# Six native fp32 gate panels in a hybrid mixer block, instead of three native and three split

## The reference, cut to what matters

```python
h = rms_norm(x, g_mix)
proj = h @ w_in                                   # 1024 x 5060
u_ssm, q, k, v, qi, ki, wi, qm, gates = jnp.split(proj, offs, axis=-1)
...
y_ssm = s5_branch(...); y_dsa = dsa_branch(...); y_mem = memory_branch(...)
g_s, g_d, g_m = jnp.split(jax.nn.sigmoid(gates), 3, axis=-1)
merged = g_s * (y_ssm @ w_up_ssm) + g_d * (y_dsa @ w_up_dsa) + g_m * (y_mem @ w_up_mem)
x = x + merged @ w_out
x = x + hier_moe(rms_norm(x, g_ffn), ...)         # 32 experts, top 2
```

## Time and profile before

| | |
|---|---|
| median of 3 runs | 2053.33 us (2052.51 to 2055.39) |
| the profiled execution, its time | 2054.06 us |
| its span, first to last instruction | 2052.2 us |
| TensorE busy | 1892.3 us |
| VectorE busy | 1189.7 us |
| ScalarE busy | 820.0 us |
| mean granted clock of TensorE | 0.967 |

### The profile page before, as it was taken

The page is one execution under the profiler, slowest core; times in us unless marked ns, Lnnn a source line. Parts: engine busy times, 40 slices in busy tenths (PEclk is TensorE's granted clock), DMA queues, the critical chain, the costliest instruction groups (busy, mean ns, idle before and its releaser), DMA issues.

```text
span 2052.2 us, 29797 instructions
## 1 busy us (share of the span) xinstructions
PE 1892.3 (92%) x12272; PEld 1419.6 (69%) x12272; DVE 1189.7 (58%) x1495; ACT 820.0 (40%) x1016; POOL 90.0 (4%) x79
## 2 busy tenths in 40 slices
PE   7988998877787787799999999999999999999998
PEld 5335666544444444588898778888888898788887
DVE  6998745533333343654578566555655688385554
ACT  4215442222222121543357475333533368465332
POOL 2670000000000000000000000000000000000000
PEclk9999999899999889899999999999999999999999
DMA  7223337799999999555454444554564544455643
GB/s 251 90 82 123 124 105 303 300 420 420 420 420 420 421 419 416 188 185 194 150 178 168 163 144 160 190 205 144 205 205 167 182 166 148 140 168 175 211 164 103
DMA packets 160440, 453.40 MB, mean 221 GB/s; under 512 B 9600, under 2 KB 21120, under 8 KB 135728
## 3 DMA queue, kind: packets, MB, share of 16 engines
q1 hardware_dynamic: 158480, 447.65, 59.2%
q10 hardware_dynamic: 1616, 3.24, 0.5%
q0 software_dynamic: 208, 0.59, 0.1%
HBM read 544.78 MB, written 1.05 MB: 266 GB/s over the span
## 4 chain that ended last, share of the span: by engine, by line
PE 72%; DMA 17%; DVE 7%; ACT 2%; issue 1%; POOL 1%; SPq 0%; ACTq 0%; DVEq 0%; POOLq 0%
PE ps L992 23%; PE ps L1002 17%; PE ps L1001 17%; DMA ring<-in_w_down 12%; DMA ring<-in_w_up 4%; PE ps L1160 3%; PE ps L1465 2%; PE ps L1483 2%; PE ps L1444 1%; DVE xn L2454 1%; PE ps L1128 1%; PE ps L1129 1%; DVE W L2459 1%; DVE W L2461 1%; DVE xn L2448 1%
## 5 line engine op out<-in xcount | busy, mean ns | idle before, releaser
L2270 DVE TENSOR_TENSOR w_lo<-raw,w_hi 128x2048 fp32r<-128x2048 f32 (+2 forms) x153 | 336.1, 2208 | 135.4 <-ACT w_hi L1757 128.3
L1757 ACT ACTIVATE w_hi<-raw 128x2048 fp32r<-128x2048 f32 (+2 forms) x153 | 281.6, 1849 | 226.8 <-PE ps L992 189.9
L1002 PE MATMUL ps<-w_hi,a_lo 128*128 128x512 f32 (+1 forms) x984 | 371.5, 378 | 0.0
L992 PE MATMUL ps<-w_hi,a_hi 128*128 128x512 f32 (+1 forms) x936 | 356.8, 381 | 0.2 <-DVEq L2310 0.2
L1001 PE MATMUL ps<-w_lo,a_hi 128*128 128x512 f32 (+1 forms) x928 | 349.5, 377 | 0.0
L1465 PE MATMUL ps<-ring,W 128*32 128x256 f32 x3008 | 191.0, 402 | 60.2 <-DMA ring<-in_w_up 60.2
L1002 PEld LDWEIGHTS ps<-w_hi,a_lo 128*128 128x128 f32 x984 | 185.1, 188 | 34.5
L992 PEld LDWEIGHTS ps<-w_hi,a_hi 128*128 128x128 f32 x936 | 176.2, 188 | 33.2 <-issue 2.1
L1001 PEld LDWEIGHTS ps<-w_lo,a_hi 128*128 128x128 f32 x928 | 174.8, 188 | 30.8
L1465 PEld LDWEIGHTS ps<-ring,W 128*32 128x32 f32 x3008 | 95.8, 114 | 142.0 <-DMA ring<-in_w_up 68.8
L2270 DVE TENSOR_TENSOR y_lo<-raw,y_hi 128x2048 fp32r<-128x2048 f32 x51 | 116.9, 2291 | 51.9 <-ACT y_hi L1757 49.1
(11 more groups left out here) (436 smaller groups left out, 2857.3 us busy)
## 6 DMA issues: line engine op xcount, KB each, us to landing
ring<-in_w_gate SPq DMA_DIRECT2D x94, 1024.0 KB
ring<-in_w_up SPq DMA_DIRECT2D x94, 1024.0 KB
ring<-in_w_down SPq DMA_DIRECT2D x94, 1024.0 KB
raw<-in_w_in SPq DMA_DIRECT2D x56, 1024.0 KB, 5.1
raw<-in_ffn_w_gate SPq DMA_DIRECT2D x44, 1024.0 KB, 5.1
raw<-in_ffn_w_up SPq DMA_DIRECT2D x44, 1024.0 KB, 5.1
raw<-in_ffn_w_down SPq DMA_DIRECT2D x40, 1024.0 KB, 5.9
raw<-in_w_out SPq DMA_DIRECT2D x9, 1024.0 KB, 5.1
```

What stands on the lines that cost most here:

```text
L992: return released(pe.matmul(dst, a, b, skip_group_check=True, **kw))
L1002: return pe.matmul(dst, a_l, b_h, start=False, stop=final, skip_group_check=True)
L1757: act.activation(E.hi_view(name, ahead), E.raw_view(name, ahead), ACT.Copy).then_inc(hi_split, 1)
L2270: tt(E.lo_view(name, ahead), E.raw_view(name, ahead), E.hi_view(name, ahead).bitcast(F32), ALU.subtract)\
```

## The change

gate(1), gate(4) and gate(5) are computed natively, from raw weights and `a_full`. Their six units are neither rounded nor subtracted, and `g_hi`, `g_lo` and the signal `gate_rows` are gone. The panels of `w_out` stay split.

```diff
-PRE_SPLIT = [(n, kh) for n in [("gate", c) for c in (1, 4, 5)] + [("wo", c) for c in range(2)] for kh in range(2)]
+PRE_SPLIT = [(n, kh) for n in [("wo", c) for c in range(2)] for kh in range(2)]
...
-    mark("gate_rows", "hi", "lo")
...
-        g_hi, g_lo = y_lo[:, 0:2].rearrange("p a k s -> p (a k) s"), a_lo
...
             def gate(c):
                 fills = [("gate", c, t) for t in range(2)]
-                if (("gate", c), 0) in PRE_SPLIT:
-                    pe.wait_ge(done["gate_rows"], nth("gate_rows", "lo"))
-                    rows_panel(halves(("gate", c)), fills, (g_hi, g_lo))
-                else:
-                    raw_rows(halves(("gate", c)), fills)
+                raw_rows(halves(("gate", c)), fills)
...
-            act.wait_ge(unit_used, E.unit_value(("vm", 1)) + 1)
-            act.wait_ge(done["turned"], nth("turned", ("x", 1, 1)))
-            act.activation(g_hi, a_full[:, :, :], ACT.Copy).then_inc(done["gate_rows"], 1)
-            act.wait_ge(done["gate_rows"], nth("gate_rows", "hi"))
-            hi1((("gate", 1), 0))
-            hi1((("gate", 1), 1))
             for h in range(2):
                 act.wait_ge(done["gelu_in"], nth("gelu_in", h))
...
-            hi1((("gate", 4), 0))
-            hi1((("gate", 4), 1))
             gate(2)
...
-            hi1((("gate", 5), 0))
             exponentials("dsa", 1, probs, 0, 8)
-            hi1((("gate", 5), 1))
             gate(4)
...
-            dve.wait_ge(done["gate_rows"], nth("gate_rows", "hi"))
-            tt(g_lo[:, :, :], a_full[:, :, :], g_hi.bitcast(F32), ALU.subtract).then_inc(done["gate_rows"], 1)
-            dve.wait_ge(done["gate_rows"], nth("gate_rows", "lo"))
-            lo1((("gate", 1), 0))
-            lo1((("gate", 1), 1))
             dve.wait_ge(done["rstd"], nth("rstd", "heads1"))
...
-            lo1((("gate", 4), 0))
-            lo1((("gate", 4), 1))
             normalised("dsa", 0, 4, probs, 0)
             selected(1)
             row_maxima("dsa", 1, 4, 0.125, key_bias, probs, 0)
-            lo1((("gate", 5), 0))
             normalised("dsa", 1, 4, probs, 0)
             attended("dsa", 0, 1)
-            lo1((("gate", 5), 1))
```

More of the change, by code:

```diff
@@ L65 @@
 SIGNALS = ("meansq rstd rows gained turned_hi turned ssm_act ssm_vec ssm_params ssm_weights trig angle rope_angle "
-           "rope_trig u_rows scanned rotated mixed gate_rows gelu_in gelu evacuated heads heads_turned values "
+           "rope_trig u_rows scanned rotated mixed gelu_in gelu evacuated heads heads_turned values "
            "relued maxed exped probs probs_turned branch gates residual route_in route silu hidden "
```

## The result

The changed kernel takes 2063.52 us, median of 5 runs (2062.87 to 2064.75), the kernel before 2053.75 us, median of 5: a ratio of 1.0048, 95% interval 1.0033 to 1.0062. It is slower by 9.8 us, 6.8 to 12.7 by the interval; 8.2 us were forecast, and the range of 2058.0 to 2065.5 us holds the median.

The account below looks back on a forecast made before the run. TensorE was taken to bound the kernel from 159 to 322 us; three native panels add 2.67 + 2.77 + 2.79 = 8.2 us, removed work nothing, giving 2061.5 us for the median, range 2058.0 to 2065.5.

Parts of the forecast that it names:

- TensorE sets the stage, and the delay goes to the end: From 159 to 322 us a TensorE microsecond more is one later; the expert stage can't absorb the 8.2 us.
- The case in which the delay is swallowed: Rival: the expert stage, bound by transfers from 373 us, takes the delay in; 2053.3 us, chance 0.06.
- The price of a panel: gate(1), gate(4), gate(5) native at 13.79 us each against 11.12, 11.02, 11.00 split: 8.2 us more.
- The estimate from the Trainium skill: Panels priced from the pages: native 13.8 us, split 10.4 us, so 3.5 us a panel and 10.4 in all.
- The removed work is worth nothing: 13.2 us less on ScalarE and 15.9 us less on VectorE bring no gain, as neither is awaited there.
- The clock: Rival on slips at TensorE's gaps: one vanishing gives 2060 us, two added 2065; two or more added, chance 0.06.
- The other side (faster): Rival: VectorE sets the pace at 192.60 and 230.95 us, up to 11.3 us back; 2050.2 us, chance 0.02.
- gate(0)'s row of 15.62 us: Upper bound for a native panel: gate(0) at a granted clock of 0.55 at first, costing 1.8 us more.
- gate(4) follows dense work: Reason for 13.79 us, the full-clock row: gate(1), gate(4) and gate(5) all follow dense TensorE work.
- the first scores' slip: Slow clock at 196 to 200 us, 16 matmuls in 3.53 us against 2.00; its vanishing would return 1.5 us.
- its four gaps: TensorE waits of 1.9, 1.5, 2.0 and 0.5 us, each ended by a ScalarE copy, expected to stay.
- the least that can be told from none: For the whole kernel: a change under 0.2% (4.1 us) can't be told from none.

Follow-up runs that it names:

- filled pair: Kernel before and changed kernel, both with extra unread TensorE products at the same six gaps: split 2047.59 us, native 2057.03 us (11 runs each).
- experiment 2: Kernel before with gate(1), gate(4), gate(5) native but all split work kept and waited for: 2063.05 us, ratio 1.0048.
- experiment 3: Kernel before, gate(4) and gate(5) using gate(1)'s rounded units, their own four neither rounded nor subtracted, still three products: 2053.97 us, ratio 0.9998.
- experiment 5: The changed kernel run again beside more runs of the kernel before: 2063.11 us (5 runs) beside 2053.39 (21 runs), ratio 1.0051.
- plain pair: The kernel before and the changed kernel, both without extra products in TensorE's gaps: 2053.75 and 2063.52 us, ratio 1.0048.
- experiment 8: Kernel before with four more units split (second and third branch's projections up): 2050.98 us, ratio 0.9984; with gaps filled too, 2045.81 us, ratio 0.9965.
- experiment 4: Changed kernel with seven extra TensorE products in some gaps (turned heads, dsa_scores(0), routing's ranks): 2063.46 us, ratio 1.0045.
- experiment 1: Kernel before with gate(4) alone native, its two units neither rounded nor subtracted: 2056.60 us (11 runs) beside 2053.98, ratio 1.0016.
- experiment 7: Kernel before and changed kernel, each with extra TensorE products at the same six gaps: split 2047.59 us, ratio 0.9979; native 2057.03 us, ratio 1.0017.

## Why the prediction was right, point by point

- **TensorE sets the stage, and the delay goes to the end: right.** TensorE is 9.7 us late at gate(5)'s end, and so is the first expert load; the token rows are 10.9 us late, the products behind the experts 10.9, the end 10.8. The case in which the delay is swallowed is out.
- **The price of a panel: right to 0.1 us, the sum short by a quarter of a microsecond.** 13.74, 13.84 and 13.74 us against 13.79 forecast. What the sum left out is the hand-over: gate(1) and gate(5) start 0.2 and 0.1 us later after the start of the group ahead of them when they are native (6.90 for 6.72 us, 1.75 for 1.66); gate(4) does not. From the start of glu to gate(1)'s end it is 17.84 and 20.64 us, from the turned memory heads to gate(5)'s end 12.66 and 15.49, and gate(4) 11.02 and 13.84: 2.80 + 2.83 + 2.82 = 8.45 us (glu and heads start at 174.76 and 251.35 before, at 175.04 and 258.19 after). The filled pair shows 8.4. The estimate from the Trainium skill ("FP8 and Floating Point Precision", TensorE Precision Notes, and "TensorE: Matmul & The Clock Gate", Back-to-back issue gap), 10.4 us, was too high: it counts a split product at 215.8 ns where gate(4)'s 48 take 11.02 us, 230 ns each. That section of the Trainium skill gives this figure for the gap of a single matmul, and about 131 ns for a sustained stream of weight loads and matmuls of 512 columns; no run here shows 131 ns.
- **The removed work is worth nothing: right,** by the list of waits and by experiments 2 and 3. The slack grew as forecast: the turned q heads are ready at 182.9 us and asked for at 195.68, 12.8 us instead of 9.3; the first half's probabilities at 231.2 and 234.99, 3.8 instead of 3.4.
- **The clock: the term that was mis-sized.** The forecast let the slips stand as they were, with one either way. In the profiled pair the changed kernel lost 0.3 us more in gate(0), 0.9 in the scores and 1.2 in the routing, 2.4 us beside the panels' 8.45; that makes the 10.8. With the gaps filled, the stretch from gate(0) to w_out shows the panels' price alone. So the excess in this stretch is the clock's. Set against its length at the full clock, 161.73 us split and 170.13 native, each plain profile has a loss of its own:

  | profile | gate(0) to the last turned part | over the full clock |
  |---|---|---|
  | before, split | 164.31 | 2.6 |
  | experiment 3, split | 164.77 | 3.0 |
  | experiment 2, native | 172.10 | 2.0 |
  | changed, native | 173.95 | 3.8 |
  | experiment 5, native | 174.10 | 4.0 |

  The two executions of the changed kernel in this table are the slowest and all but the slowest of their five runs, and that of experiment 2 is the fastest of its five, so the table shows what can happen and not an average. By the means the plain pair is 10.2 us apart, with a standard error of about 0.4 us (estimated from the scatter of the runs), which is more than the panels' 8.45; the filled pair is 8.5 apart. So the changed kernel does lose more to the clock, by some 2 us, in the stretch and in the routing together, and the forecast had no term for it beyond one slip either way. Why it does stays open. The native form alone doesn't bring it: the smallest loss is that of a native execution, and in experiment 8 a split one, whose TensorE does up to gate(4) what the kernel before does, had all three groups of scores slow.
- **The other side (faster): out.** Experiment 3 took 9.1 us from VectorE and 7.6 from ScalarE, and no gain shows (at most 2.3 us by its interval).
- **Smaller slips of the prediction.** It sets gate(0)'s row of 15.62 us, with its drain, against 13.79 from start to start; from start to start gate(0) took 15.46, so the low clock cost 1.7 us there and not 1.8. It says that gate(4) follows dense work; gate(4) follows 16 small matmuls of 2.00 us behind a gap of 1.97, and in experiment 4 the low clock reached into it (14.26 us). It prices the first scores' slip at 1.5 us; experiment 1 without it was 0.9 us shorter there, because the next gap grew from 1.49 to 2.08 us. One of its four gaps is ended by the relu (L1913), not by a copy. And it takes 4.1 us as the least that can be told from none, where experiment 8 told 2.4 us with 11 runs beside 21.

## What to carry to other kernels

Three rounded products (fp32r) cost TensorE 0.69 us for a 128x128 by 128x512 block and a native fp32 product 0.86 us: leaving the split out frees the other engines and charges TensorE a quarter more, so where TensorE sets the pace it can pay only if a rounding or remainder is what TensorE waits for. Ask at each handover who arrives last; here VectorE was 3.4 and 9.3 us early, and splitting four more units gained 2.4 us. When a forecast rests on rows of one execution, look for stretches of theirs at the lower clock, and give each one a price both ways, with what the next gap gives back. To compare two forms, take a stretch that ran at the full clock in both.

## What the runs showed of the hardware that was not expected

- The granted clock fell under or just ahead of small matmuls behind TensorE gaps of 1.5 to 2.0 us in some executions and not in others: 16 score matmuls took 2.00 us or up to 3.79 us. Where a gap was filled with products that nobody reads, the score matmuls behind it took 2.00 us in all five profiles with extra products; in experiment 4 the clock fell at the next open gap.
- Filling can backfire: products put in after the clock has fallen run at the slow rate (eight instructions of 512 columns in 4.82 us for 3.70, and in the routing in 5.26) and may end after the wait that they fill: in the native kernel of experiment 7 TensorE no longer waited for the last read-out and came to it later, relative to the one before, than the split kernel did (6.26 us for 4.97).
